# Gelus ahead of the copies of the same point, and block ends without a GpSimd drain, in a 512-token transformer kernel

## The chip, the cores and the metric

The kernel runs on one core of a Trainium2 chip. The metric is the device time of one execution in microseconds (us), as the median over runs. The profile is taken from one further execution of the same program.

## The reference, cut to what matters

The reference is two blocks over one sequence of 512 tokens of width 1024, all in float32. The first block ends with a product-key expert layer: for each token and each of 8 heads it picks 16 experts, and adds for each expert one row of a table, weighted by a gelu of an inner product with another row. The second block is two hybrid layers (stick-breaking attention and a sparse attention, both gated), each with an input projection, an output projection and a layer norm.

```python
def chunk(hc):                                   # peer_ffn, per 128 tokens
    ...
    ue = peer_u[experts]
    ve = peer_v[experts]
    act = jax.nn.gelu(jnp.einsum('td,thkd->thk', hc, ue).astype(jnp.float32), approximate=False)
    return jnp.einsum('thk,thkd->td', (g * act).astype(ve.dtype), ve)

def hybrid_layer(x, w_in, w_out, ln_g, ln_b, rel_bias, topk):
    proj = jnp.einsum('bsd,dn->bsn', x, w_in)
    qA, kA, vA, gA, qB, kB, vB, gB, qI, kI, wI = jnp.split(proj, SPLIT_POINTS, axis=-1)
    ...
    mix = jnp.concatenate([oA * jax.nn.silu(gA), oB * jax.nn.silu(gB)], axis=-1)
    y = jnp.einsum('bsm,md->bsd', mix, w_out)
    return layer_norm(ALPHA * x + y, ln_g, ln_b)
```

## The kernel before, in words

The kernel is written engine by engine: each stage is one `nc.Block()`, inside which SyncE, GpSimd (POOL), TensorE (PE), ScalarE (ACT) and VectorE (DVE) each run a list of instructions in the order written and meet only at semaphores. At the end of a block all engines meet at a barrier. `nc.Block()` drains every engine there; for GpSimd this includes its queue of software-described DMAs. After the block, GpSimd clears the semaphores of the stage.

The 512 tokens are four tiles of 128. An expert row is a GATHER: GpSimd issues one indirect DMA (L1335) that brings 128 rows of 8 KB, 1 MB in all (the u half and the v half of one expert for each token), into one of 10 slots. There are 128 gathers per tile.

`peer_stage` (its block is L1386) handles the 256 gathers of tiles 0 and 1 with inner products on DVE, gelus on ACT and weighted sums on PE. Its GpSimd program issues ten gathers more, those with which tile 2 begins, so that they are under way when the next stage starts.

`group_stage` (L1854) runs the two hybrid layers for one group of tiles: group 0 is tiles 0 and 1, group 1 is tile 2, group 2 is tile 3. Attention needs only earlier tokens, whose keys and values the earlier groups have stored in memory. While a group's layers run, the expert rows of the next group's tile are worked off beside them, in the BACKGROUND: group 0 does tile 2's 128 rows, group 1 does tile 3's, group 2 has none. The order is set out by hand. `layer_points` lists points of the layer with weights, and `Background.at` says how many rows must be done at each point. At a point DVE's `rows` runs for each row `dot` (L2442), `add` for the row five back (L2456), and at each fourth row `weigh` (L2448), which needs the gelu. GpSimd gathers again into a slot once its row has been added. ACT's `gelus(point, done)` takes the lots of four inner products that are due by that point; where at least one is due it loads the gelu table, waits for DVE's `dotted`, computes four columns, and loads the table with exp and ln again (L2258). Where none is due, it issues nothing.

PE writes the projections into two banks by turns. Each is a job with a number; ACT waits for the job in `finished` (`proj_done`) and copies it out (`proj_copied`). PE needs the copy of the job two before to start a job. The jobs of a layer are the index keys kI, two index queries qI, the stick values v0, a pair of heads, the gates g0, pairs, the sparse values v1, a pair, the gates g1, the transposed mix, pairs. The weights come in blocks of 512 KB through a ring of six (L1874), all issued by SyncE in order; block n+6 is loaded when block n's job is done. The output of a layer is L2204, the transposes of its input are L2043, the copies of v are L2292, of the gates L2338, of the index scores L2301.

Of the kernel before, what the change touches and what calls it, by code (L numbers as in the profile page):

```python
# [1338 lines left out]
def peer_stage(nc, A, m, h_t, nat):  # L1339
# [19 lines left out]
    with ctx:  # L1359
# [23 lines left out]
        expert_done = sem("expert_done")  # L1383
        shifted_ready, exp_done, norm, gates_ready = sem("shifted_ready"), sem("exp_done"), sem("norm"), sem("gates_ready")

        with nc.Block() as block:  # L1386
            @block.sync
            def _(sp):
                for h in range(HEADS):
# [390 lines left out]
def group_stage(nc, A, m, number, out):  # L1780
# [36 lines left out]
    with ctx:  # L1817
# [33 lines left out]
        squared = sem("squared")  # L1851
        dotted, gelu_done, weighed = sem("dotted"), sem("gelu_done"), sem("weighed")

        with nc.Block() as block:  # L1854
            @block.sync
            def _(sp):
                def load_block(n):
# [390 lines left out]
            def _(act):  # L2248
                def gelus(point, done):

                    ready = min(bg.at[point], bg.rows) // bg.LOT
                    for lot in range(done, ready):
                        act.wait_ge(dotted, bg.LOT * (lot + 1))
                        if lot >= bg.RING:
                            act.wait_ge(weighed, lot - bg.RING + 1)
                        nc.scalar.activation(acts[:, lot % bg.RING, :], dots[:, lot % bg.RING, :], ACT.Gelu).then_inc(gelu_done, 1)
                    if ready > done:
                        nc.scalar.preload_act_table_set("natural_log_exp_and_others")  # L2258
                    return max(done, ready)

                def finished(job):
                    n = job_at[job]
                    act.wait_ge(proj_done, n + 1)
                    return ps[:, n % 2, :]
# [12 lines left out]
                def copy_index_keys(l):  # L2277
                    bank = finished((l, "kI"))
                    if searched:
                        nc.scalar.activation(weight[:, :, :], bank[:, NQ:NQ + NT * HEADS].rearrange("p (t h) -> p t h", t=NT), ACT.Copy)  # L2280
                    if keeps and l:
                        act.wait_ge(kept, 48 * l)
                    nc.scalar.activation(key_i[:, OLD:OLD + NQ], bank[:, 0:NQ], ACT.Copy).then_inc(proj_copied, 1)
# [4 lines left out]

                def copy_values(l, half, done):
                    for t in tiles:  # L2290
                        bank = finished((l, f"v{half}", t))
                        nc.scalar.activation(values[half][:, t, :], bank, ACT.Copy).then_inc(proj_copied, 1)  # L2292
                        done = gelus((l, f"v{half}", t), done)
                    return done

                def rectify(l, n):
# [32 lines left out]
                def gates(l, half, done):  # L2329

                    if half == STICK and searched:
                        act.wait_ge(summed, SCORES * (l + 1))
                    if half == SPARSE:
                        act.wait_ge(gate_ready, NT * (2 * l + 1))
                    for n, t in enumerate(tiles):
                        count = NT * (2 * l + half) + n
                        bank = finished((l, f"g{half}", t))
                        nc.scalar.activation(mix[:, n, half * HALF:(half + 1) * HALF], bank, ACT.Copy)  # L2338
                        nc.scalar.activation(share[:, n, :], bank, ACT.Exp, scale=-1.0).then_inc(proj_copied, 1)
                        act.wait_ge(proj_copied, job_at[l, f"g{half}", t] + 1)  # L2340
                        nc.scalar.activation(share[:, n, :], share[:, n, :], ACT.Ln, bias=1.0).then_inc(gate_step, 1)
                        act.wait_ge(gate_step, 2 * count + 1)
                        nc.scalar.activation(share[:, n, :], share[:, n, :], ACT.Exp, scale=-1.0).then_inc(gate_step, 1)
                        done = gelus((l, f"g{half}", t), done)
                    return done

                def sparse_weights(l, u):
# [21 lines left out]
                done = 0  # L2369
# [4 lines left out]
                done = gelus((0, "first"), done)  # L2374
                inverse_roots(0)
                for l in range(LAYERS):
                    done = gelus((l, "first"), done)
                    for t in tiles:
                        for n in range(2):
                            copy_input(l, t, n)  # L2380
                    done = gelus((l, "start"), done)
                    copy_index_keys(l)
                    done = gelus((l, "kI"), done)
                    for n in range(2):
                        copy_index_queries(l, n)
                        done = gelus((l, "qI", n), done)
                    done = copy_values(l, STICK, done)
                    for n in range(SCORES):
                        rectify(l, n)
# [5 lines left out]
                    done = gelus((l, "soft0"), done)  # L2395
                    done = gates(l, STICK, done)
                    for u in range(PAIRS):
                        copy_pair(l, u + 1)
                        done = gelus((l, "stick", u, 0), done)
                        stick_weights(l, u)  # L2400
                        done = gelus((l, "stick", u, 1), done)
                        if u + 1 < PAIRS:
                            softplus(l, u + 1)
                        else:
                            done = copy_values(l, SPARSE, done)
                        done = gelus((l, "stick", u, 2), done)
                        done = gelus((l, "stick", u, 3), done)
# [378 lines left out]
```

## Time and profile before

| What | us |
|---|---|
| median of 3 runs | 3009.46 (3005.42 to 3011.15) |
| the profiled execution, its own time | 2989.41 |
| its span | 2987.6 |
| last DVE work of the peer stage to the first DMA issue of group 0 | 1604.04 to 1621.62 |
| group 0 | 1621.6 to 2166.0 |
| group 1 | 2175.7 to 2674.5 |
| group 2 | 2674.8 to the end |

Times inside the profile count from the span's start. A timeline row gives the start, the duration, the engine and line, the operation, and in square brackets how long the engine had been idle before and what ended that. A row by windows gives the busy time of each engine in a stretch, the granted TensorE clock as a share of full speed, and the share in which the core's 16 DMA engines were busy.

### The profile page before, as it was taken

What the parts mean: (1) busy time and instruction counts of PE and PEld (TensorE: products, weight loads), DVE (VectorE), ACT (ScalarE), POOL (GpSimd) and SP (SyncE); (2) the same over time, 40 slices, a digit from 0 to 9 for tenths busy, and PEclk for the clock granted to TensorE, in tenths of its full rate; (3) what the DMA queues carried; (4) which work ended last, traced back from release to release, by engine and by line L of the source; (5) the groups of instructions that cost most, each with busy time, mean ns of one, the idle gap of its engine ahead of it and who ended that gap; (6) DMA issues with size and microseconds to landing.
All of it is one profiled execution on the core that took longest, in us unless ns stands there. A gap on an engine that the chain in (4) does not pass through costs nothing. (4 is left out here: it accounts for less than half of the span.)

```text
span 2987.6 us, 30208 instructions
## 1 busy us (share of the span) xinstructions
PE 2399.5 (80%) x9721; PEld 1601.4 (54%) x9721; DVE 1746.2 (58%) x3652; ACT 906.0 (30%) x1730; POOL 985.4 (33%) x691
## 2 busy tenths in 40 slices
PE   6997999869876888898885986798547457649897
PEld 4776878758653443343332664475336335427574
DVE  3444311031118988888974588587759878864251
ACT  3443222233312222222221334143224314323232
POOL 2332555343213344344442234324313432320101
PEclk9998999979988999999897997899768778769998
DMA  4321333223108999999999898899789999965553
GB/s 156 99 67 50 95 99 102 82 80 127 56 23 318 397 417 408 416 411 399 402 413 368 315 383 347 339 372 398 299 331 375 414 406 392 389 254 219 215 190 140
DMA packets 255851, 803.85 MB, mean 269 GB/s; under 512 B 18302, under 2 KB 138518, under 8 KB 190183
## 3 DMA queue, kind: packets, MB, share of 16 engines
q0 software_dynamic: 73728, 536.90, 44.4%
q1 hardware_dynamic: 181991, 265.35, 25.3%
q8 instruction: 63, 1.03, 0.1%
q14 instruction: 69, 0.57, 0.0%
HBM read 793.36 MB, written 14.07 MB: 270 GB/s over the span
## 5 line engine op out<-in xcount | busy, mean ns | idle before, releaser
L1335 POOL DMA_INDIRECT gathered<-in_peer_rows,experts x436 | 534.7, 1226 | 912.8 <-DVE x_res L2456 623.4
L1446 PE MATMUL peer_banks<-gathered,peer_diags 128*128 128x512 f32 x720 | 344.4, 635 | 57.7 <-ACT peer_diags L1506 57.6
L78 PE MATMUL group_banks<-group_x_t,group_ring 128*128 128x128 f32 (+1 forms) x2016 | 340.7, 332 | 15.9 <-ACT group_x_t L2268 8.4
L2442 DVE CUSTOM_DVE_ANT_0 gathered<-gathered,late_nat 128x1024 f32<-128x1024 f32 x256 | 316.2, 1238 | 39.6 <-DMA gathered<-in_peer_rows,experts 27.4
L78 PEld LDWEIGHTS group_banks<-group_x_t,group_ring 128*128 128x128 f32 x2016 | 308.3, 209 | 45.9 <-ACT group_x_t L2268 10.8
L2456 DVE SCALAR_TENSOR_TENSOR x_res<-gathered,group_weights,x_res 128x1024 f32<-128x1024 f32 x256 | 329.6, 1288 | 2.5
L1446 PEld LDWEIGHTS peer_banks<-gathered,peer_diags 128*128 128x128 f32 x720 | 144.6, 204 | 248.8 <-issue 248.8
L2082 PE MATMUL group_banks<-group_ring,group_x_t 128*128 128x512 f32 x512 | 235.1, 615 | 21.9 <-DMA group_ring<-in_weights 21.8
L1609 DVE CUSTOM_DVE_ANT_0 peer_product<-gathered,early_nat 128x1024 f32<-128x1024 f32 x180 | 214.9, 1223 | 40.6 <-DMA gathered<-in_peer_rows,experts 40.5
L1446 PE MATMUL peer_banks<-peer_early_gathered,peer_diags 128*128 128x512 f32 x304 | 150.8, 650 | 43.1 <-ACT peer_diags L1506 43.1
L1499 ACT ACTIVATE peer_acts<-peer_dots 128x2 f32<-128x2 f32 x128 | 26.0, 203 | 517.3 <-DVE peer_dots L1609 517.2
L2082 PEld LDWEIGHTS group_banks<-group_ring,group_x_t 128*128 128x128 f32 x512 | 98.9, 198 | 144.7 <-issue 118.5
L2001 POOL TENSOR_TENSOR group_bias<-group_bias,group_keep 128x768 f32<-128x768 f32 (+1 forms) x24 | 50.2, 2105 | 327.6 <-DVE group_keep L2511 237.0
L1335 POOL DMA_INDIRECT peer_early_gathered<-in_peer_rows,experts x76 | 83.1, 1093 | 206.5 <-PE peer_banks L1446 117.6
L1446 PEld LDWEIGHTS peer_banks<-peer_early_gathered,peer_diags 128*128 128x128 f32 x304 | 62.5, 210 | 126.1 <-issue 125.9
L2204 PE MATMUL group_banks<-group_ring,group_mix_t 128*128 128x512 f32 x256 | 125.2, 652 | 5.8 <-ACT group_mix_t L2366 4.1
L2171 PE MATMUL group_banks<-ident,group_work 128*128 128x128 f32 x160 | 31.1, 351 | 122.1 <-ACT group_work L2354 122.1
L78 PE MATMUL peer_banks<-peer_h_t,peer_w 128*128 128x512 f32 x256 | 115.1, 605 | 8.0 <-DMA peer_w<-in_w_pq 8.0
L95 POOL TENSOR_TENSOR mixer_wq_parts<-mixer_wq,mixer_wq_parts 128x1024 fp32r<-128x1024 f32 x24 | 57.7, 2406 | 191.4 <-ACT mixer_wq_parts L526 125.2
L944 DVE TENSOR_TENSOR merge_gated<-merge_gates,merge_banks 128x512 f32<-128x512 f32 x16 | 11.0, 688 | 161.5 <-PE merge_banks L78 161.5
L2043 PE MATMUL group_banks<-ident,x_res 128*128 128x128 f32 x64 | 16.2, 428 | 107.1 <-DVE x_res L2480 81.3
L78 PEld LDWEIGHTS group_banks<-group_values,group_work 128*128 128x128 f32 x640 | 89.3, 220 | 23.4 <-ACT group_work L2361 16.7
(324 smaller groups left out, 4244.6 us busy)
## 6 DMA issues: line engine op xcount, KB each, us to landing
group_ring<-in_weights SPq DMA_DIRECT2D x270, 512.0 KB, 7.6
mixer_wq<-in_w_in SPq DMA_DIRECT2D x24, 512.0 KB, 4.1
mixer_wk<-in_w_in SPq DMA_DIRECT2D x24, 512.0 KB, 4.3
peer_w<-in_w_pq SPq DMA_DIRECT2D x8, 1024.0 KB, 20.0
gathered<-in_peer_rows,experts POOLq DMA_INDIRECT x436, 11.1
diff_wv<-in_w_in SPq DMA_DIRECT2D x8, 512.0 KB, 4.1
conv_wb<-in_w_in SPq DMA_DIRECT2D x8, 512.0 KB, 4.1
merge_w<-in_w_conv_out SPq DMA_DIRECT2D x8, 512.0 KB, 3.7
```

The lines of the kernel that those rows point to most:

```text
L78: last = nc.tensor.matmul(out, lhsT, rhs, start=n == 0, stop=n == len(pairs) - 1)
L95: return engine.tensor_tensor(low, whole, high.bitcast(F32), ALU.subtract)
L1335: nc.gpsimd.indirect_dma_start(row_buffer(m, r), None, A["peer_rows"], bass.IndirectOffsetOnAxis(ap=at, axis=0))\
L1446: last = nc.tensor.matmul(ps[:, ACC[unit % 2] + half, :], diags[:, r % DIAGS, :], row_buffer(m, r)[:, D + half * BANK:D + (half + 1) * BAN ...
L1499: nc.scalar.activation(acts[:, lot % RING, :], dots[:, lot % RING, :], ACT.Gelu).then_inc(gelu_done, 1)
L1609: nc.vector.tensor_tensor_reduce(out=product[:, r % 2, :], in0=row_buffer(m, r)[:, 0:D], in1=nat[t // 2][:, t % 2, :], scale=1.0, scalar=0 ...
L2001: nc.gpsimd.tensor_tensor(bias[:, n % 2, :, :], bias[:, n % 2, :, :], keep[:, :].unsqueeze(1).to_broadcast([P, 2, SC]), ALU.add)\
L2082: made = nc.tensor.matmul(bank, x_t[:, 2 * b + c, local(t)], w[:, c * HALF:(c + 1) * HALF], start=b == 0 and c == 0, stop=b == 3 and c == 1)
L2171: made = nc.tensor.transpose(ps[:, pair_banks(u) + e, b * P:(b + 1) * P], work[:, u % 2, e, b * P:(b + 1) * P], m.ident[:, :])
L2204: made = nc.tensor.matmul(ps[:, 2 + 2 * n + half, :], mix_t[:, c, local(t)], w[:, half * HALF:(half + 1) * HALF], start=c == 0, stop=c == ...
L2442: nc.vector.tensor_tensor_reduce(out=row, in0=row, in1=m.late_nat[:, t % 2, :], scale=1.0, scalar=0.0, op0=ALU.mult, op1=ALU.add, accum_ou ...
L2456: nc.vector.scalar_tensor_tensor(out=m.x[:, t, :], in0=row_buffer(m, r)[:, D:2 * D], scalar=weights[:, lot % bg.RING, n % bg.LOT:n % bg.LO ...
```

## The change

Two block openings get `no_gpsimd_drain=True`: that of the peer stage and that of the group stage. At their end GpSimd is no longer drained; the other engines are drained as before, and a barrier made of semaphores alone joins them. In ACT's program of the group stage, at each point that has both a copy of a projection and gelus, the gelus are taken first. The calls and their counts are the same, and so are all waits.

```diff
-        with nc.Block() as block:                       # peer_stage
+        with nc.Block(no_gpsimd_drain=True) as block:
...
-        with nc.Block() as block:                       # group_stage
+        with nc.Block(no_gpsimd_drain=True) as block:
...
                 def copy_values(l, half, done):
                     for t in tiles:
+                        done = gelus((l, f"v{half}", t), done)
                         bank = finished((l, f"v{half}", t))
                         nc.scalar.activation(values[half][:, t, :], bank, ACT.Copy).then_inc(proj_copied, 1)
-                        done = gelus((l, f"v{half}", t), done)
...
                         count = NT * (2 * l + half) + n          # gates
+                        done = gelus((l, f"g{half}", t), done)
                         bank = finished((l, f"g{half}", t))
...
-                        done = gelus((l, f"g{half}", t), done)
                     return done
...
+                    done = gelus((l, "kI"), done)
                     copy_index_keys(l)
-                    done = gelus((l, "kI"), done)
                     for n in range(2):
+                        done = gelus((l, "qI", n), done)
                         copy_index_queries(l, n)
-                        done = gelus((l, "qI", n), done)
...
                     for u in range(PAIRS):
+                        done = gelus((l, "stick", u, 0), done)
                         copy_pair(l, u + 1)
-                        done = gelus((l, "stick", u, 0), done)
                         stick_weights(l, u)
```

## Rows read from the trace of the kernel before

**Rows 1.** The page: engines' busy us (share, instructions); GpSimd's DMA queue: packets, MB, share.

```profile
PE 2399.5 (80%) x9721; PEld 1601.4 (54%) x9721; DVE 1746.2 (58%) x3652; ACT 906.0 (30%) x1730; POOL 985.4 (33%) x691
q0 software_dynamic: 73728, 536.90, 44.4%
```

**Rows 2.** Windows: us, busy by engine, PE clock, DMA share, GB/s.

```profile
1604.05:1621.60 17.55, 0.00 (x0) 0.00 (x0) 0.00 (x0) 0.00 (x0) 0.00 (x0) 0.62 0.70 289
1616.40:1621.60 5.20, 0.00 (x0) 0.00 (x0) 0.00 (x0) 0.00 (x0) 0.00 (x0) 0.50 0.04 16
2168.40:2175.70 7.30, 0.00 (x0) 0.00 (x0) 0.00 (x0) 0.00 (x0) 0.02 (x1) 0.50 0.66 269
1621.60:2166.00 544.40, 439.38 (x1712) 298.03 (x1712) 401.83 (x674) 190.29 (x321) 187.50 (x134) 0.87 0.90 350
2175.70:2674.50 498.80, 304.34 (x1456) 218.48 (x1456) 398.21 (x615) 168.04 (x261) 168.27 (x126) 0.75 0.93 369
```

**Rows 3.** Timeline from the peer stage into group 0.

```profile
1602.82 1.22 DVE L1628 TENSOR_TENSOR x_res<-x_res,peer_banks 128x1024 f32<-128x1024 f32 x1 [7.39 <-PE peer_banks L1446]
1621.62 0.82 SPq L1874 DMA_DIRECT2D group_ring<-in_weights  x2
1628.85 2.74 DVE L2480 SCALAR_TENSOR_TENSOR x_res<-x_res,group_inv,group_affine 128x512 f32<-128x512 f32 x4 [2.01 <-DMA group_affine<-in_final_g]
```

**Rows 4.** Timeline from group 0 into 1, and from group 1 into 2.

```profile
2167.48 0.94 POOL L1335 DMA_INDIRECT gathered<-in_peer_rows,experts  x1 [0.30 <-issue]
2670.55 3.92 DVE L2456 SCALAR_TENSOR_TENSOR x_res<-gathered,group_weights,x_res 128x1024 f32<-128x1024 f32 x3
2674.76 1.28 ACT L2370 ACT_TABLE_LOAD   x1 [7.22 <-PEq L1854]
```

**Rows 5.** ACT's timeline after v0 in group 0, layer 0, then layer 1.

```profile
1671.30 0.60 ACT L2292 ACTIVATE group_values<-group_banks 128x512 f32<-128x512 f32 x1 [6.27 <-PE group_banks L2082]
1673.44 1.28 ACT L2258 ACT_TABLE_LOAD   x1
1674.73 0.38 ACT L2301 ACTIVATE group_work<-group_banks 128x256 f32<-128x256 f32 x1
...
1945.23 0.60 ACT L2292 ACTIVATE group_values<-group_banks 128x512 f32<-128x512 f32 x1 [3.45 <-PE group_banks L2082]
1945.86 0.38 ACT L2301 ACTIVATE group_work<-group_banks 128x256 f32<-128x256 f32 x1
```

**Rows 6.** PE's timeline: the same stretches of group 0, then v0 in group 1.

```profile
1677.77 9.84 PE L78 MATMUL group_banks<-group_x_t,group_ring 128*128 128x256 f32 x32
1688.36 0.92 PE L2113 MATMUL group_banks<-group_q_t,group_k_t 64*128 64x256 f32 x8 [0.75 <-ACT group_k_t L2311]
1948.38 7.17 PE L78 MATMUL group_banks<-group_x_t,group_ring 128*128 128x256 f32 x32
1956.30 0.92 PE L2113 MATMUL group_banks<-group_q_t,group_k_t 64*128 64x256 f32 x8 [0.75 <-ACT group_k_t L2311]
2219.43 6.93 PE L2082 MATMUL group_banks<-group_ring,group_x_t 128*128 128x512 f32 x12 [10.72 <-DMA group_ring<-in_weights]
```

**Rows 7.** DVE's timeline: its waits for a gelu and for index scores.

```profile
1652.81 0.16 DVE L2448 TENSOR_TENSOR group_weights<-group_acts,gates 128x4 f32<-128x4 f32 x1 [9.37 <-ACT group_acts L2256]
1675.15 0.35 DVE L2490 TENSOR_SCALAR group_score<-group_work,group_weight 128x256 f32<-128x256 f32 x1 [13.80 <-ACT group_work L2301]
1795.10 0.16 DVE L2448 TENSOR_TENSOR group_weights<-group_acts,gates 128x4 f32<-128x4 f32 x1 [9.90 <-ACT group_acts L2256]
2228.54 0.16 DVE L2448 TENSOR_TENSOR group_weights<-group_acts,gates 128x4 f32<-128x4 f32 x1 [21.48 <-ACT group_acts L2256]
2349.41 0.16 DVE L2448 TENSOR_TENSOR group_weights<-group_acts,gates 128x4 f32<-128x4 f32 x1 [3.48 <-ACT group_acts L2256]
```

**Rows 8.** ACT: the gelu due after g1, and one that waits for DVE.

```profile
1801.67 0.20 ACT L2256 ACTIVATE group_acts<-group_dots 128x4 f32<-128x4 f32 x1
2494.05 0.21 ACT L2256 ACTIVATE group_acts<-group_dots 128x4 f32<-128x4 f32 x1 [1.16 <-DVE group_dots L2442]
```

## The prediction

> **What bounds the kernel now.** I read the page first. PE is busy for 80% of the span and no other engine for more than 58% [rows 1], but shares over the span say nothing of the places that this change touches. So I cut the span into stages by windows. The change acts in two of them and at their edges: group 0 (544.4 us, PE busy 439, DVE 402, DMA share 0.90) and group 1 (498.8 us, PE 304, DVE 398, DMA 0.93) [rows 2]. Nobody is full in either. The reader is to see two lists that hold each other up in turns, DVE with the background rows and PE with the layer, over DMA engines that are busy for all but a tenth of the time. A microsecond saved on one engine counts only if the other is waiting for it, and if the DMAs behind it have room.
>
> Then the timeline at the edges. After the peer stage's last DVE instruction (1602.82 + 1.22 = 1604.04) nothing starts before 1621.62 [rows 3]. In these 17.55 us all engines stand still and the DMAs move 289 GB/s x 17.55 = 5.1 MB: five of the ten early gathers, done by about 1616.4, after which the engines are idle for another 5.2 us [rows 2]. So the block end waits for the gathers. From group 0 to 1, GpSimd's last issue ends at 2168.42 and the next work is at 2175.7, with two gathers in flight [rows 2, 4]. From group 1 to 2 no gather is in flight: DVE ends at 2674.47 and ACT begins at 2674.76, 0.3 us later [rows 4]. The same block end costs 17.6, 7.3 and 0.3 us: the drain costs what the outstanding gathers take, and a barrier without it costs 0.3 us.
>
> Last the timelines of ACT, DVE and PE inside the groups, lot by lot. In ACT's list some gelus stand behind a copy for which PE is not ready. DVE, which needs the gelu for its next add, then waits for PE's projection: 9.4, 9.9, 21.5 and 3.5 us are four of these waits [rows 7].
>
> **The change part by part.**
>
> *Which calls matter.* From the weights of the points I worked out where lots fall due. Of 64 gelus (32 a group), nine in group 0 and seven in group 1 belong to a call that moves: qI, v0, g0, v1, g1 in group 0; v0, g0, g1, kI, v1 in group 1. None is ever due at the first point of a stick pair, so that edit is empty. The count of table loads doesn't change: each of these gelus still has a load before and one after it, 1.28 us each [rows 5].
>
> *Block end, peer to group 0.* The barrier comes at 1604.04 + 0.3, so 17.3 us earlier. The start is not gained in full: the layer begins when the gain row (the third 512 KB load) has landed, 7.2 us after the start with empty DMA queues [rows 3]. Now 5.1 MB of gathers stand beside it. If the two queues take turns by packet, gathers in pieces of 536.90 MB / 73728 = 7.3 KB [rows 1] and weights in rows of 4 KB, the 1.57 MB of loads get a third of some 414 GB/s (5.1 MB in the 12.3 us to 1616.4) and take 7.6 us more; at equal bytes 3.8 more; behind the whole backlog 12.3 more. I take 6.5: the row lands at 1604.4 + 7.2 + 6.5 = 1618.1 instead of 1628.9. Gain 10.7, of which I keep 10 since the early part of the layer then runs closer to its weights. Bounds 5 and 13.5.
>
> The Trainium skill has a rule here (DMA: Bandwidth & Descriptors, Queues, rings and completion order): each DMA engine goes round its queues and switches only between whole packets of some 9 to 17 descriptors. If gather packets are the bigger ones, the rule speaks for the low end, a gain near 5 instead of 10; the rows of before show no such start beside a backlog.
>
> *Block end, group 0 to 1.* Start at 2168.42 + 0.3 instead of 2175.7: 6.9 us. But in group 1 PE waits at v0 for its weights until 2219.43 (10.72 us) [rows 6], so there the DMA queue sets the time, and it gains only the time in which the DMAs now idle: 0.34 x 7.3 = 2.5 us at the edge [rows 2] and a little of the start after it. I take 3, bounds 0 and 6.9. From group 1 to 2 there is nothing to gain.
>
> *Gelus of v0 first.* In group 0, layer 0, ACT copies v at 1671.30, loads tables round a gelu, and only then starts the index scores at 1674.73. In layer 1 the lot falls before the last copy, and the scores start at 1945.86, right behind the copy of 1945.23 [rows 5]. That is the new order, already in the trace. To PE's next product with keys it is 1688.36 - 1671.30 = 17.1 us in layer 0 and 1956.30 - 1945.23 = 11.1 in layer 1 [rows 5, 6]: 3 us are the gelu pair, 2.7 the slower clock of the pair product behind the gap (9.84 against 7.17 us [rows 6]). Gain 6.0; PE sets the time there until the stick loop. In both layers of group 1 the gelu also stands between the copy and the scores, but PE's clock is already low behind the wait for weights, so I take the pair only, 2.8 each. Sum 11.6, bounds 5 and 12.
>
> *Gelus of qI first, group 0.* DVE's 9.4 us wait goes, but its next is one of 13.8 us for the scores [rows 7]: the stall moves there. 0.
>
> *Gelus of g1 first.* In group 0, layer 0, DVE's 9.9 us wait goes. Late next is the following lot: its gelu is at 1801.67 [rows 8], behind both g1 copies and unmoved, and DVE now reaches it first. DVE used it at 1804.7, so 3 us remain. In group 1 the wait is 3.5 us [rows 7] and the next lot is in time, but the DMAs are full there; I take 2. Sum 5, bounds 0 and 8.
>
> *Gelus of g0, v1, kI first.* Here DVE can be the late one. In group 1, layer 1, the gelu of g0 waits for dots until 2494.05 [rows 8]; the copy and its three activations, done before it so far, now come behind it, about 4 x 0.6 = 2.5 us later for the next pair's copy (durations as in rows 5). DVE has its searches before it needs that pair, so I expect no one to wait for it. At v1 and kI no one reads the copy before the gelu's wait is over. I take a loss of 1, bounds 0 and 5.
>
> The skill (ScalarE: Activation LUTs, What ACT_TABLE_LOAD costs) gives 2.66 us for a switch of table set with its drain. Here the gelu ran 1.3 us after its load began. By the page's figure the pair moved out of the v0 stretch would be 5.3 instead of 2.8 and the sum some 7 us larger; the trace doesn't agree, and I stay with 1.28.
>
> *Sum.* 10 + 3 + 11.6 + 5 - 1 = 28.6. With DMAs at 0.90 and 0.93 a part of what is gained inside the groups is given back as waits for rows or weights; of the 18.6 behind the first edge I take off a tenth, 2. That is 27 us from 2989, 0.9%, and from the median of 3009.5 (the profiled execution was 20 us shorter than it) 2982.5.
>
> **The rivals.**
>
> *The DMAs take it back.* DVE freed early at v0 issues gathers early, just when PE's weights are due. In group 1, layer 0, DVE stands still for 21.5 us before 2228.54 [rows 7] and no gather is issued; that is when the late weights land [rows 6]. With one or two 1 MB gathers (2.5 us each) in front of them at each of the four v0 stages, and the first edge worth 5: 5 + 0 + 11.6 - 10 + 3 = 10 us, time 3000. For it: the wait of 10.72. Against it: group 0 has no such wait in this trace.
>
> *Slower.* The same crowding in full: a PE wait of 10.7 us at each of four v0 stages is 43 us against 28.6 gained: 14 us slower, 3024. It decides from a stall of 7 us per stage on. Against it: DVE gets only one or two adds further before it waits for the scores, so it can't free more slots.
>
> *The change doesn't do what it says.* If the barrier without a drain still waits for the gathers GpSimd has issued, the edges give 0. The gelus alone are 15.6, less 2: 14 us, 2995.5. Against it: the 0.3 us of the last edge; only GpSimd's own drain has a reason to look at the DMA queue.
>
> *More than added up.* PE's granted clock averages 0.87 and 0.75 in the groups [rows 2]; with fewer gaps it may stay up, as in the 2.7 us above. With both edges near their upper bounds (13.5 and 6.9) the sum is 36, and with some clock 42: 2967.
>
> **How the numbers follow.** Forecast as summed, 2973 to 2992: 0.58. DMAs take it back, about 3000: 0.14. Edges give nothing, 2995: 0.08. More, about 2967: 0.07. Slower: 0.06. No change to speak of, by several of these taking each other away: 0.07. A measurement of this kernel can tell 0.2%, 6 us, from no change. So faster 0.87, same 0.07, slower 0.06. The range goes from 2967 to 3001; below it is half of the fourth case, above it the cases of no change and slower.
>
> **What the changed profile would show.** Right: group 0 begins within 1 us of the last DVE instruction of the peer stage while DMAs are at 1.0, its first L2480 comes 12 to 16 us after that, group 1 starts within 1 us of GpSimd's last issue; L2301 follows L2292 at once in group 0, layer 0; of DVE's four waits for L2256 in rows 7 three are gone and the second is under 1 us or moved to the next lot with up to 7. Wrong: the edges are still 17 and 7 us; L2082 waits for the ring in group 0, or for more than 11 us in group 1; ACT's copies L2338 and L2292 appear after long waits for DVE with PE standing behind them.

## The result and the profile after

The changed kernel takes 2990.07 us (median of four runs, 2986.57 to 2993.60) against 3009.07 us for the kernel before on the same chip. The ratio is 0.9947 with an interval of 0.9935 to 0.9960, which is 16 us faster (12 to 20). I had forecast 2983.0, that is 27 us off the median. The direction and the range hold; by the ratio 11 of the 27 us did not come, by the medians 8. The profiled execution took 2986.57 us, only 3 less than the one of before, but its peer stage, whose instructions no edit changes, ended 10 us later (1614.2 against 1604.0). In the second profile of the changed kernel it ended at 1608.4, so stages are compared from there on.

The page and three windows of the kernel after (columns as in [rows 1] and [rows 2]):

```profile
PE 2393.8 (80%) x9721; PEld 1600.9 (54%) x9721; DVE 1743.3 (58%) x3652; ACT 905.7 (30%) x1730; POOL 985.2 (33%) x691
```

```profile
1614.00:1630.60 16.60, 0.00 (x0) 0.00 (x0) 5.91 (x15) 6.65 (x10) 0.00 (x0) 0.63 1.01 413
1614.30:2161.60 547.30, 436.32 (x1712) 295.31 (x1712) 400.75 (x674) 190.34 (x321) 184.78 (x134) 0.87 0.91 356
2163.80:2668.20 504.40, 303.99 (x1456) 218.96 (x1456) 399.99 (x615) 167.34 (x261) 165.55 (x127) 0.75 0.93 369
```

The page shows nothing: busy times and counts are those of [rows 1] within 0.3%. The windows show that group 0 now includes the landing of the gathers, at a DMA share of 1.01 and 413 GB/s, and takes 547.3 us where it took 544.4, and that group 1 takes 504.4 where it took 498.8. So what the two edges give, 17.3 and some 8 us, is in part paid inside the groups. How much of such a difference is chance between two executions is seen in the table below.

The timeline from the peer stage into group 0, and from group 0 into 1:

```profile
1613.01 1.22 DVE L1628 TENSOR_TENSOR x_res<-x_res,peer_banks 128x1024 f32<-128x1024 f32 x1 [7.38 <-PE peer_banks L1446]
1614.58 1.28 ACT L2370 ACT_TABLE_LOAD   x1 [7.98 <-PEq L1386]
1614.60 0.82 SPq L1874 DMA_DIRECT2D group_ring<-in_weights  x2
...
1629.92 2.74 DVE L2480 SCALAR_TENSOR_TENSOR x_res<-x_res,group_inv,group_affine 128x512 f32<-128x512 f32 x4 [10.13 <-DMA group_affine<-in_final_g]
...
2163.13 0.94 POOL L1335 DMA_INDIRECT gathered<-in_peer_rows,experts  x1 [0.30 <-issue]
2163.53 1.28 ACT L2370 ACT_TABLE_LOAD   x1 [10.44 <-PEq L1854]
2163.84 0.82 SPq L1874 DMA_DIRECT2D group_ring<-in_weights  x2
```

The 17.55 us of [rows 3] are 0.35 us (1614.23 to 1614.58), and the 7.3 us of [rows 4] are gone: ACT starts while GpSimd is still finishing its last issue. The gain row now ends DVE's wait 15.3 us after the first load is issued (1629.92 - 1614.60); it was 7.2 us in [rows 3]. So 8.1 of the 17.3 us come back and 9.1 stay.

ACT and PE round the copy of v in group 0, layer 0 (before: [rows 5, 6]):

```profile
1671.81 0.60 ACT L2293 ACTIVATE group_values<-group_banks 128x512 f32<-128x512 f32 x1 [3.45 <-PE group_banks L2082]
1672.43 0.38 ACT L2301 ACTIVATE group_work<-group_banks 128x256 f32<-128x256 f32 x1
```

```profile
1671.70 3.32 PE L2073 MATMUL group_banks<-group_key_i,group_query_i 64*128 64x256 f32 x16
1674.95 7.17 PE L78 MATMUL group_banks<-group_x_t,group_ring 128*128 128x256 f32 x32
1682.88 0.92 PE L2113 MATMUL group_banks<-group_q_t,group_k_t 64*128 64x256 f32 x8 [0.75 <-ACT group_k_t L2311]
```

The scores follow the copy at once, and the pair product takes 7.17 us, not 9.84; the granted clock over it is 1.00, where it was 0.72. From L2073 to L2113 it is 11.2 us, where it was 17.2.

To see where the rest went I measured stages in the traces, from the starts of instructions: the peer stage's last DVE instruction, the block's start, and in each layer the first L2043 (x), the first L2073 (scores) and the first L2204 (out). Line numbers move by up to six in some kernels. "Before, again" and "change, again" are second profiled executions. The other columns are experiments 1, 2, 3, 5 and 6, described below. All in us:

| stage | before | before, again | change | change, again | drains only | gelus only | qI back | two places | hold |
|---|---|---|---|---|---|---|---|---|---|
| peer end to start | 17.6 | 17.6 | 0.3 | 0.3 | 0.3 | 17.6 | 0.3 | 0.3 | 0.3 |
| group 0: start to x | 8.0 | 7.9 | 16.2 | 16.3 | 16.2 | 8.5 | 16.3 | 16.2 | 16.4 |
| layer 0: x to scores | 41.5 | 41.0 | 41.0 | 42.6 | 42.6 | 39.0 | 41.3 | 42.6 | 41.4 |
| scores to out | 188.4 | 188.5 | 174.4 | 174.2 | 185.9 | 173.6 | 173.5 | 173.7 | 177.4 |
| out to x | 36.7 | 36.4 | 36.7 | 37.3 | 36.6 | 37.3 | 37.3 | 37.5 | 37.1 |
| layer 1: x to scores | 48.8 | 53.7 | 56.8 | 57.2 | 53.7 | 57.2 | 49.0 | 49.1 | 48.9 |
| scores to out | 178.1 | 177.9 | 178.4 | 178.4 | 176.2 | 178.4 | 178.5 | 179.5 | 183.5 |
| out to group 1 | 52.5 | 54.0 | 45.6 | 45.7 | 44.7 | 54.4 | 44.6 | 45.9 | 45.5 |
| group 1, layer 0: x to scores | 38.4 | 40.7 | 43.4 | 45.5 | 41.8 | 40.8 | 44.9 | 42.2 | 35.1 |
| all of group 1 | 499.1 | 503.2 | 505.0 | 501.2 | 503.8 | 502.9 | 510.5 | 504.8 | 497.5 |
| group 2 | 312.8 | 316.9 | 316.4 | 317.0 | 316.2 | 316.4 | 316.2 | 316.5 | 317.3 |
| sum from peer end | 1383.6 | 1397.1 | 1370.6 | 1370.2 | 1376.3 | 1385.4 | 1367.5 | 1366.1 | 1365.2 |

Two stages got shorter for good (the edges; scores to out in layer 0, by 14), and one got longer: x to scores in layer 1 of group 0. It takes 57 to 58 us in all four traces with qI's gelus first and no hold (58.3 in experiment 4, which has no column) and 48.8 to 49.1 in seven of the other nine.

The two others, before again and drains only, take 53.7 us without any wait for weights. There it is PE's clock (windows of before, then of before again, PE alone):

```profile
1917.40:1931.30 13.90, 13.90 (x67) 1.00 0.95 348
1919.20:1935.90 16.70, 16.70 (x65) 0.83 0.66 224
```

The same 64 products of the index queries take 14.06 us at a granted clock of 1.00 and 16.92 at 0.83, and the 16 before them 5.19 and 6.72. What made the clock rise later in these two executions the traces do not say.

Here is PE in that stage and what DVE and GpSimd do, in the kernel after:

```profile
1903.75 15.75 PE L78 MATMUL group_banks<-group_x_t,group_ring 128*128 128x256 f32 x64
1919.33 5.31 PE L2082 MATMUL group_banks<-group_ring,group_x_t 128*128 128x512 f32 x12
1929.33 10.30 PE L2082 MATMUL group_banks<-group_ring,group_x_t 128*128 128x512 f32 x20 [4.68 <-DMA group_ring<-in_weights]
1939.56 3.32 PE L2073 MATMUL group_banks<-group_key_i,group_query_i 64*128 64x256 f32 x16
```

```profile
1905.94 0.16 DVE L2448 TENSOR_TENSOR group_weights<-group_acts,gates 128x4 f32<-128x4 f32 x1 [1.23 <-ACT group_acts L2256]
...
1940.71 0.35 DVE L2490 TENSOR_SCALAR group_score<-group_work,group_weight 128x256 f32<-128x256 f32 x1 [26.26 <-ACT group_work L2301]
```

```profile
1901.49 1.68 POOL L1335 DMA_INDIRECT gathered<-in_peer_rows,experts  x1 [0.66 <-DVE x_res L2456]
1903.84 1.68 POOL L1335 DMA_INDIRECT gathered<-in_peer_rows,experts  x1 [0.66 <-DVE x_res L2456]
1907.70 1.68 POOL L1335 DMA_INDIRECT gathered<-in_peer_rows,experts  x1 [2.18 <-DVE x_res L2456]
1910.04 1.68 POOL L1335 DMA_INDIRECT gathered<-in_peer_rows,experts  x1 [0.66 <-DVE x_res L2456]
...
1914.72 0.94 POOL L1335 DMA_INDIRECT gathered<-in_peer_rows,experts  x1 [0.66 <-DVE x_res L2456]
```

DVE, which no longer waits for its gelu, frees a slot every 2.3 us, but for one pause of 3.9, and GpSimd fills each at once with a gather of 1 MB. PE then waits 4.68 us for a weight block of v0, where it had not waited in either trace of before, and DVE, which has run through its rows, waits 26.3 us for the scores. In the second trace of the change the wait is longer, while the stage takes 57.2 us, nearly the same:

```profile
1925.92 10.52 PE L2082 MATMUL group_banks<-group_ring,group_x_t 128*128 128x512 f32 x20 [6.27 <-DMA group_ring<-in_weights]
```

Whether the gelus of qI cause it is the third experiment's question.

### The profile page after: what moved, and what is told of

Same layout as the page of the kernel before. It is cut to its first block and busy times, and to the rows that moved or that the text cites. A ratio compares the mean times of both kernels' runs of the same rounds, so it can differ in the third digit from the quotient of the medians.

```text
span 2984.8 us, 30216 instructions
## 1 busy us (share of the span) xinstructions
PE 2393.8 (80%) x9721; PEld 1600.9 (54%) x9721; DVE 1743.3 (58%) x3652; ACT 905.7 (30%) x1730; POOL 985.2 (33%) x691
## 5 line engine op out<-in xcount | busy, mean ns | idle before, releaser
L78 PE MATMUL group_banks<-group_x_t,group_ring 128*128 128x128 f32 (+1 forms) x2016 | 335.7, 329 | 16.3 <-ACT group_x_t L2268 8.4
L2442 DVE CUSTOM_DVE_ANT_0 gathered<-gathered,late_nat 128x1024 f32<-128x1024 f32 x256 | 319.9, 1252 | 38.4 <-DMA gathered<-in_peer_rows,experts 31.9
L78 PEld LDWEIGHTS group_banks<-group_x_t,group_ring 128*128 128x128 f32 x2016 | 304.0, 206 | 44.9 <-ACT group_x_t L2268 10.8
L2082 PE MATMUL group_banks<-group_ring,group_x_t 128*128 128x512 f32 x512 | 236.2, 616 | 32.3 <-DMA group_ring<-in_weights 32.3
L2082 PEld LDWEIGHTS group_banks<-group_ring,group_x_t 128*128 128x128 f32 x512 | 99.5, 200 | 155.6 <-issue 117.2
L2204 PE MATMUL group_banks<-group_ring,group_mix_t 128*128 128x512 f32 x256 | 124.1, 648 | 4.6 <-ACT group_mix_t L2366 4.1
L78 PEld LDWEIGHTS group_banks<-group_values,group_work 128*128 128x128 f32 x640 | 91.0, 224 | 23.8 <-ACT group_work L2361 16.6
L1609 DVE CUSTOM_DVE_ANT_0 peer_product<-peer_early_gathered,early_nat 128x1024 f32<-128x1024 f32 x76 | 90.8, 1224 | 18.1 <-DMA peer_early_gathered<-in_peer_rows,experts 18.1
```

The lines of the kernel that those rows point to most:

```text
L78: last = nc.tensor.matmul(out, lhsT, rhs, start=n == 0, stop=n == len(pairs) - 1)
L1609: nc.vector.tensor_tensor_reduce(out=product[:, r % 2, :], in0=row_buffer(m, r)[:, 0:D], in1=nat[t // 2][:, t % 2, :], scale=1.0, scalar=0 ...
L2082: made = nc.tensor.matmul(bank, x_t[:, 2 * b + c, local(t)], w[:, c * HALF:(c + 1) * HALF], start=b == 0 and c == 0, stop=b == 3 and c == 1)
L2204: made = nc.tensor.matmul(ps[:, 2 + 2 * n + half, :], mix_t[:, c, local(t)], w[:, half * HALF:(half + 1) * HALF], start=c == 0, stop=c == ...
L2442: nc.vector.tensor_tensor_reduce(out=row, in0=row, in1=m.late_nat[:, t % 2, :], scale=1.0, scalar=0.0, op0=ALU.mult, op1=ALU.add, accum_ou ...
```

## The experiments

Each kernel was timed beside the kernel before on the same chip, and a ratio is to that; 0.001 is 3 us. Differences between ratios of two experiments carry the errors of both.

**1. The edges alone.** The kernel before, with this and nothing else:

```diff
-        with nc.Block() as block:                       # peer_stage, group_stage
+        with nc.Block(no_gpsimd_drain=True) as block:
```

> Only the two block openings are changed; the gelus stay behind the copies. My theory: the edge into group 0 gains 17 us and gives 7.5 back because the gain row lands late beside the backlog of gathers, the edge into group 1 gains 7 to 8 us, of which PE's wait for weights at v0 takes a part. So 11 to 15 us faster than before, ratio about 0.9955, and group 0 opens within 1 us of the peer stage's last DVE instruction. Rival (the gelus carry the change): 5 us or less. Rival (the gelus first cost more than they give, by gathers issued ahead of the weights): this kernel is faster than the whole change, 18 us or more.

Measured: 2990.82 us, 0.9957 (0.9942 to 0.9972), 13 us faster. This is the sum of my two edge terms (10 and 3). The table has the edges at 0.3 us and the later gain row, and scores to out of layer 0 within 3 us of before (185.9 against 188.4), as it should be with the gelus where they were. The rival by which the change doesn't do what it says is out.

**2. The gelus alone.** The kernel after with both block openings as before.

> Only the order of gelus and copies is changed; blocks drain GpSimd as before. My theory: the terms of the gelus were oversized. What the v0 stretch of group 0, layer 0, gives (6 us) stays, but at qI in layer 1 DVE runs ahead, its gathers go out before the weights of v0, and PE waits for them: 3 to 7 us faster, ratio about 0.998. Rival (the forecast's sum): 14 us, 0.9953. Rival (crowding outweighs): no gain or slower, 1.000 or more.

Measured: 2994.54 us, 0.9959 (0.9946 to 0.9973), 12 us faster. My expectation of 3 to 7 was too low, and the forecast's sum, which stood there as the rival, is inside the interval. The 14 us in layer 0 of group 0 are there (173.6), and so is the 57.2 us stage in layer 1: it belongs to the gelus and not to the drain. The two parts alone add up to 25 us; together they gave 16 (12 to 20), and 18 in a second measurement. With errors of some 4 us on each, a loss of a few us between them is likely and no more than that is shown.

**3. The whole change, but qI's gelus behind qI's copies.**

```diff
                     for n in range(2):
-                        done = gelus((l, "qI", n), done)
                         copy_index_queries(l, n)
+                        done = gelus((l, "qI", n), done)
```

> The whole change, except that the gelus of the two qI points stay behind their copies. Only two lots move, both in group 0, lots 1 and 17. Theory of crowding: in layer 1 DVE again waits 8 to 9 us for lot 17 and PE's wait of 4.7 us for the ring at v0 shrinks to under 2 us; the time is 2 to 5 us below the whole change. Rival (PE's wait comes from the whole program having moved up against its DMAs, not from these gathers): the wait stays at 4 us or more and the time is that of the whole change.

Measured: 2978.64 us, 0.9908 (0.9893 to 0.9922): some 12 us better than the change (0.9947, 0.9935 to 0.9960; with the two intervals, 6 to 18), from taking one of its lines back. I had expected 2 to 5. The same stretch as above, which in this execution begins 5.9 us earlier:

```profile
1898.17 14.06 PE L78 MATMUL group_banks<-group_x_t,group_ring 128*128 128x256 f32 x64
1912.07 13.90 PE L2082 MATMUL group_banks<-group_ring,group_x_t 128*128 128x512 f32 x32
1925.90 3.32 PE L2073 MATMUL group_banks<-group_key_i,group_query_i 64*128 64x256 f32 x16
```

```profile
1907.51 0.16 DVE L2448 TENSOR_TENSOR group_weights<-group_acts,gates 128x4 f32<-128x4 f32 x1 [8.69 <-ACT group_acts L2256]
```

```profile
1897.95 1.68 POOL L1335 DMA_INDIRECT gathered<-in_peer_rows,experts  x1 [0.66 <-DVE x_res L2456]
1909.27 1.68 POOL L1335 DMA_INDIRECT gathered<-in_peer_rows,experts  x1 [9.64 <-DVE x_res L2456]
```

DVE's wait is back, at 8.7 us, and with it 11.3 us between the starts of two gathers. In the kernel after six gathers are issued from 1901.49 to 1914.72; in the same stretch here (1895.6 to 1908.8) there are two, and the next four come some 7.5 us later in the layer than in the kernel after. Four gathers are 4.2 MB, some 10 us at 410 GB/s. SyncE's issues of the weight blocks of this stretch, in the kernel after and then here:

```profile
1903.92 9.02 SPq L1874 DMA_DIRECT2D group_ring<-in_weights  x2
1913.94 6.39 SPq L1874 DMA_DIRECT2D group_ring<-in_weights  x3
```

```profile
1898.35 7.34 SPq L1874 DMA_DIRECT2D group_ring<-in_weights  x2
1907.56 5.51 SPq L1874 DMA_DIRECT2D group_ring<-in_weights  x3
```

Each pair and each three begins within 0.5 us of the same place in the layer. The second block of the pair is 1.3 us later in the kernel after, but not in its second trace, where PE's wait is even longer. They are asked for at the same time and land later. PE's 20.3 us for v0 (5.31, a wait of 4.68, 10.30) are 13.9 without a wait: 4.7 us are the wait, 1.7 come from the granted clock after it (0.85 against 1.00), and 1.4 more lie before L2082; together the 7.8 us of the table's stage. The last 1.4 are a lower clock too (0.89) and not the gathers' work: in the second trace of the change that product runs at 1.00, and PE waits 1.6 us longer for the same block instead. The idle engine was doing something useful: it held back the DMAs.

Two sets of waits from 1600 to 2700 us (engine, tile and line, releaser: us in total, times, longest), first of the kernel after, then of this one:

```profile
PE group_banks L2082 <- DMA group_ring<-in_weights: 32.3, 5, 15.1
DVE group_weights L2448 <- ACT group_acts L2256: 16.6, 6, 5.8
DVE gathered L2442 <- DMA gathered<-in_peer_rows,experts: 31.9, 30, 2.4
DVE group_score L2490 <- ACT group_work L2301: 77.1, 4, 26.3
```

```profile
PE group_banks L2082 <- DMA group_ring<-in_weights: 30.9, 5, 16.4
DVE group_weights L2448 <- ACT group_acts L2256: 32.3, 6, 9.1
```

DVE waits 16 us longer for gelus, and the kernel is the faster one. PE's waits for weights add up to nearly the same, though: the wait in group 0 is gone, and those of group 1 are longer. Of this kernel's 8 us a good part is lost again in its own profile, in group 1 (510.5 us against 505.0 and 501.2; layer 1 takes 51.0 us from x to scores where the change took 46.0 and 43.8), so the profiled sum is only 3 us lower, while the ratios differ by 12. One execution of each does not settle the size; the place is settled by the five kernels below without the crowding (5, 6, 7, 10 and 11), where this stage takes 48.8 to 49.1 us.

**4. The gain row ahead of the first weights.** Whole change, with SyncE's first loads turned round.

```diff
-                for n in range(2):
-                    load_block(n)
                 sp.dma_start(affine[:, 0, :], A["final_g"].unsqueeze(0).to_broadcast([P, D])).then_inc(affine_loaded, 16)
+                for n in range(2):
+                    load_block(n)
```

> The whole change, and SyncE issues the gain row of the final norm ahead of the first two weight blocks instead of behind them. If the start of group 0 waits for that row in a queue shared with the backlog, DVE's wait at L2480 of 10.1 us falls to 3 us or less; group 2's start gains some 2.5 us too (1 MB less ahead of it). Together 4 to 9 us below the whole change. Rival (the row waits for the gathers and not for the weights ahead of it in its own queue): the wait stays above 8 us.

Measured: 2992.28 us, 0.9958 (0.9945 to 0.9971), no better than the change, though DVE's wait for the gain row fell to 2.64 us, as expected. DVE and PE at the start of group 0:

```profile
1615.48 2.74 DVE L2480 SCALAR_TENSOR_TENSOR x_res<-x_res,group_inv,group_affine 128x512 f32<-128x512 f32 x4 [2.64 <-DMA group_affine<-in_final_g]
```

```profile
1658.41 13.96 PE L2082 MATMUL group_banks<-group_ring,group_x_t 128*128 128x512 f32 x28 [10.95 <-DMA group_ring<-in_weights]
```

The layer begins 7.6 us earlier (start to x 8.6 instead of 16.2 us) and PE then waits 10.95 us for v0's weights (x to scores 56.0 instead of 41.0). The two stages together are 64.6 us; they were 57.2. What the late gain row costs is the price of the gathers' bytes, and turning the loads round only moves the stall.

**5. Only two places.** Drains off; gelus first only for v0 in group 0 and for g1 in group 0 (and at the first point of a stick pair, where none is due).

```diff
                     for t in tiles:
+                        if number == 0 and half == STICK:
+                            done = gelus((l, f"v{half}", t), done)
                         bank = finished((l, f"v{half}", t))
...
+                        if number == 0 and half == SPARSE:
+                            done = gelus((l, f"g{half}", t), done)
                         bank = finished((l, f"g{half}", t))
```

> Both block ends without the drain; the gelus go first only at v0 and g1 of group 0, and stay behind the copies everywhere else (qI, kI, g0, v1, and all of group 1). By the first four kernels the gelus earn 12 to 14 us between v0 and the output product of group 0, layer 0, and nothing that shows in group 1, where PE waits for its weights at v0. Theory: with the crowding gone from both groups the time is that of the kernel with only the qI gelus put back, or up to 4 us less: ratio 0.989 to 0.991. Rival (the moves in group 1 earn the 2.8 us twice that the forecast gave them): 4 to 6 us slower than that kernel, 0.9925.

Measured: 2972.48 us, 0.9906 (0.9887 to 0.9924). The same as experiment 3, so the gelus of qI, kI, g0, v1 and of all of group 1 bring nothing in sum by going first, or take something. The 14 us of layer 0 are all there (173.7).

**6. Hold the gathers instead of the gelus.** The whole change, and GpSimd waits at qI for PE to be through with v0's last job, so that no gather is issued beside v0's weights.

```diff
...
                         if bg.rows:
+                            if point == ("qI", 1):
+                                pool.wait_ge(proj_done, job_at[l, "v0", last] + 1)
                             done = rows((l,) + point, done)
```

> The whole change, and in every layer GpSimd holds back its gathers from the second index query's point on until the v0 product is done (a wait on proj_done in its list). Theory of crowding: what makes PE wait for the ring at v0 are gathers ahead of the weights in the DMA queues. Then PE's waits L2082 for the ring fall from 32 us to 15 or less, the stretch from the transposes to the index scores of group 0, layer 1, is back at 49 us, and the whole is 5 to 15 us below the change; DVE may wait up to 3 us per layer for its next rows. Rival (the weights are late by their own number, issued late): the waits stay at 25 us or more and the time is the same or, by DVE's waits, longer.

Measured: 2975.51 us, 0.9920 (0.9900 to 0.9941), 6 to 8 us better than the change by the ratios, with intervals that overlap. This is the cleanest test of the cause, since qI's gelus still go first here: layer 1 of group 0 is back to 48.9 us, and group 1's first layer takes 35.1 instead of 43 to 45. The waits of this kernel:

```profile
PE group_banks L2084 <- DMA group_ring<-in_weights: 13.7, 3, 7.6
...
DVE gathered L2444 <- DMA gathered<-in_peer_rows,experts: 50.9, 40, 6.5
```

PE's waits for weights fall from 32.3 to 13.7 us, and DVE's for rows rise from 31.9 to 50.9, which is more than the 3 us a layer that I had allowed. The bytes are moved, not removed: the stages after it are 3 to 5 us longer (177.4 and 183.5).

**7. Both: two places and the hold.** The edits of 5 and 6 together.

> Both of the above in one kernel: gelus first at v0 and g1 of group 0 only, and the gathers held back over v0. If the two cure the same thing in group 0 and different ones in group 1, this is the fastest: ratio 0.985 to 0.989. If holding the gathers starves DVE, it is slower than the first of this set.

Measured: 2978.08 us, 0.9922 (0.9904 to 0.9940). I had put it at 0.985 to 0.989, the fastest of all; it is not. The hold adds nothing once qI's gelus are back; if anything it costs. In group 0 they are two remedies for one stall.

**8 and 9. The change and the kernel before once more,** unedited, the latter as one profiled execution.

> The changed kernel itself, so that the others have it on their own chip, and a second profile of it. Ratio 0.993 to 0.996, 13 to 20 us faster than before. Group 0 starts within 1 us of the peer stage's last DVE instruction; between the transposes and the scores of group 0, layer 1, it takes 55 us or more again. Were that stretch 49 us this time, the crowding at qI would be chance of one execution.

> The kernel before itself, for a second profile. The first took 2989 us where its timed runs took 2999 to 3011, so it was a short execution. If the 20 us lie in stages that the change doesn't touch (the peer stage and group 2), this profile's group stages show the same durations as the first within 3 us each, edges of 17.6 and 7 us between work and work again, and the peer stage ends later than 1604 us. If they lie in groups 0 and 1, those are longer here, and the comparison stage by stage so far has understated the change.

Measured: the change 2981.33 us, 0.9940 (0.9919 to 0.9961), as the first time; its stages in group 0 repeat within 2 us, and all of group 1 within 4. The kernel before took 3003.45 us in its second profile, 14 us longer than in the one from which I predicted (2989.41). 4.9 us of it lie in x to scores of group 0, layer 1 (53.7 against 48.8), 4.1 in group 1, 4.1 in group 2. So part of what looks like a loss in a comparison of the first two traces is chance: against one profile of before that stage lost 8 us, against the other, with its lower clock, 3.

```profile
DVE group_weights L2448 <- ACT group_acts L2256: 69.8, 7, 22.9
DVE group_score L2490 <- ACT group_work L2301: 39.1, 4, 13.9
PE group_banks L2082 <- DMA group_ring<-in_weights: 23.7, 4, 11.3
```

These are the waits of before again (1600 to 2700 us); in the kernel after they are 16.6, 77.1 and 32.3. The change took 53 us of waiting for gelus from DVE, gave it 38 of waiting for scores, and gave PE 9.

**10. The hold in group 1 alone,** with the edits of 5.

```diff
-                            if point == ("qI", 1):
+                            if number == 1 and point == ("qI", 1):
```

> Both block ends without the drain, gelus first at v0 and g1 of group 0 only, and GpSimd's gathers held back over v0 in group 1 only. There the hold shortened transposes to scores from some 43 to 35 us in layer 0 and gave 1 to 4 us back after it; in group 0 it gave nothing and cost 4 to 5 us a layer behind it. Theory: 3 to 7 us below the kernel without the hold, ratio 0.988 to 0.990. Rival (DVE's waits for rows take all of it, as in both groups together): the same within 2 us, or above.

Measured: 2973.23 us, 0.9892 (0.9871 to 0.9913). PE in group 1, layer 0, of the kernel after, then of this one:

```profile
2212.73 6.82 PE L2082 MATMUL group_banks<-group_ring,group_x_t 128*128 128x512 f32 x12 [15.12 <-DMA group_ring<-in_weights]
```

```profile
2194.21 7.54 PE L2084 MATMUL group_banks<-group_ring,group_x_t 128*128 128x512 f32 x12 [7.25 <-DMA group_ring<-in_weights]
```

The wait for weights halves; it is 14.1 us in experiment 11, which differs by the hold alone. X to scores is 34.3 us against 42.2 in both kernels without the hold (5 and 11), and layer 0's scores to out, at 179.3, gives 2 to 4 of it back.

**11. The two places again,** on the same chip as 10.

> The kernel with the gelus first at v0 and g1 of group 0 only, without any hold, again, so that the hold in group 1 has it on its own chip. Ratio 0.989 to 0.992.

Measured: 2975.21 us, 0.9907 (0.9890 to 0.9924), as in 5. It differs from 10 by 2 us in the medians, and the intervals overlap for the most part; I had expected 3 to 7. The hold in group 1 is not shown to help the total: all of group 1 takes 499.6 us with it and 504.8 and 502.4 without, but the two profiles have the same sum from the peer stage's end, 1362.1. The best that I can name is the set of 3, 5, 10 and 11: 0.989 to 0.991, 28 to 32 us faster than before and 10 to 16 faster than the change.

## Why the prediction was right or wrong

For the sizes I take the mean of the two profiles of each kernel, 1390.4 and 1370.4 us from the peer stage's end: 20 us, where the medians differ by 19. The two profiles of before are 13.5 us apart, so a term of 2 or 3 us is read only where a stage repeats that well.

- **Edge, peer to group 0: right.** Forecast 10, measured 9.1. The gain row is 8.1 us later beside the backlog; I had taken 6.5, between 3.8 at equal bytes and 7.6 by turns of one packet each. The second was the nearer, and the end near 5 was not borne out. That end is where I had put the Trainium skill's rule (DMA: Bandwidth & Descriptors, Queues, rings and completion order), by which whole packets of several descriptors alternate, on the condition that the gathers' packets are the bigger ones; no trace here shows how big they are.
- **Edge, group 0 to 1: right in reason, and in size as far as it can be told.** 7.6 us at the edge. Group 1 takes it back in part: x to scores in layer 0 is 39.6 before and 44.5 after, so by that stage some 3 stay, and by all of group 1 (2 us longer) some 6. That the giving back belongs to the edge is seen in PE's wait for weights there: 10.7, 11.4 and 11.4 us in the three traces with the drain, gelus first or not, and 13.3 to 17.4 in those without drain and hold. Experiment 1 has both edge terms in one, at 13 us. They were not run apart.
- **v0 in group 0, layer 0: right.** Forecast 6.0, measured 17.2 - 11.2 = 6.0. The load of the gelu's tables still takes 1.28 us, as in [rows 5].
- **g1 in group 0: undersized.** With v0 it was to be 9; scores to out fell by 14.1, so the part behind v0 is 8 instead of 3. I had let DVE's next lot stop it as soon as DVE reached it. DVE's wait of 9.90 us is gone, and before that next lot, where I had left it 7, it waits only 1.98 (4.0 in the second trace), having waited 3.5 for rows on the way:

```profile
1795.12 0.16 DVE L2448 TENSOR_TENSOR group_weights<-group_acts,gates 128x4 f32<-128x4 f32 x1 [1.98 <-ACT group_acts L2256]
```

  What each of the two places gives was not measured apart: v0 and g1 were only run together (5).
- **"The stall moves there. 0." for the gelus of qI: the step that failed.** The stall did move, as written: DVE waits for the scores. But I priced the wait only by what DVE could do in it, and not by what GpSimd does while DVE isn't waiting. It cost 3 to 8 us in that stage (53.7 or 48.8 to 57), and taking it back gained some 12 by the ratios. My rival "the DMAs take it back" names the mechanism, though it put it at v0's gelus. I had given it 0.14, because group 0 had no wait for weights in the trace of before, and had argued that DVE gets only one or two adds further. It got four gathers further. One of my own signs of being wrong was this wait, and it came: L2082 waits for the ring in group 0, and for more than 11 us in group 1. The signs of being right came as well in the profile after (the gain row 15.3 us after the start, both groups starting within 1 us, the waits of [rows 7] at 2 us or less).
- **v0 and g1 in group 1: 5.6 and 2, measured nothing in the group's sum.** Group 1 is 501.2 us before and 503.1 after. The DMAs are at 0.93 there. In layer 0 DVE's wait of 21.5 us for the gelu [rows 7] has become one of 21.6 for the scores, since PE stands for its weights:

```profile
2220.96 0.42 DVE L2490 TENSOR_SCALAR group_score<-group_work,group_weight 128x384 f32<-128x384 f32 x1 [21.61 <-ACT group_work L2301]
```

  In layer 1 scores to out did fall, from 180.8 to 177.0 us, while x to scores rose by 1. Experiment 5 leaves those gelus where they were and is no slower.
- **g0, v1, kI: forecast -1.** No loss shows in group 0: layer 1's scores to out is 178.4 against 178.0. Experiment 5 can't tell it from zero.
- **The tenth that I took off (2): too small.** What the table has longer after the change, beside the gain row, is some 10 us, 5.7 of them in x to scores of group 0, layer 1. That the total still fell inside the range is in part luck: g1 in group 0 gave 5 us more than forecast, against 5.7 lost at qI and 7.6 that didn't come in group 1.
- **The other rivals.** Slower (3024) needed a stall of 7 us at each of four v0 stages; there is one of 4.7 (6.3 in the second trace) in group 0, and in group 1 one that is 4 to 6 us longer. "More" didn't come: the granted clock is 0.87 in group 0 and 0.75 in group 1, as before.

The trace from which I predicted was 14 us shorter than its second profile. My note that it was 20 us below the median was right, and the sum against the median stands.

Open: where the 12 us that the ratios give to experiment 3 lie, beyond the 3 to 8 of that stage (from the peer stage's end its profile is only 3 us shorter than the change, and those of 5 and 11 are 4 and 8); why PE's clock rises later in that stage in two of the executions; and where in group 1 a hold would be worth most.

## What to carry to other kernels

A wait of an engine that frees buffers for transfers is also a brake on those transfers: before you remove it, count the bytes that it lets go and look at what lands beside them. Remove such waits one at a time and measure each; here two places carried what the gelus gave in sum, and one took 8 us away in its stage, some 12 by the ratios. At block ends look for transfers in flight that nobody needs yet: a drain that waits for them costs their whole time, but they then land beside the next stage's loads, and of the 17 us here only 9 stayed.

## What I had not expected of the hardware

- With the drain, the end of the peer stage's block costs 17.6 us, of which 5.2 come after the gathers in flight have landed; without it 0.35 us, in every trace with it off.
- 4.2 MB of gathers issued some 7.5 us earlier make a weight block that was asked for at the same time land too late, by 4.7 and 6.3 us in the two traces of the change, and after the wait of 4.7 PE needs 1.7 us more for the same 32 products: 15.6 us against 13.9, at a granted clock of 0.85 after the wait.
- Two executions of the kernel before differ by 14 us in sum. 4.9 of them are a lower granted clock of PE in one stage (0.83 against 1.00 over the same product), which a comparison of single traces would have laid to the change.
